# A two-layer decoder trunk on one core: the router's logits and selection taken tile by tile

## The chip, the core and the metric

The kernel runs on one core of a Trainium2 chip (trn2). The metric is the device time of one execution in microseconds (us), and the median of several runs is compared. Names of engines in the rows: PE is TensorE's matmuls, PEld its weight loads, DVE is VectorE, ACT is ScalarE, POOL is GpSimd, SP is the engine that issues the weight loads from HBM, SPq its queue.

## The reference, cut to what matters

Two layers, each on 256 tokens of width 1024. A layer is a token mixer, a cross-attention and a mixture of experts, each followed by a residual sum and a layer norm. The change stands between the second norm and the first expert, so that only this part is quoted:

```python
x = layer_norm(DEEPNORM_ALPHA * x + xa, ln_mem_g[l], ln_mem_b[l])
gates = shared_group_router(x, router_w, router_bias)
ff = moe_ffn(x, gates, expert_w_gate[l], expert_w_up[l], expert_w_down[l])

# in shared_group_router: 16 experts in 4 groups of 4
scores = jax.nn.sigmoid((x @ router_w).astype(jnp.float32))
biased = scores + router_bias.astype(jnp.float32)
grp = biased.reshape(B, S, N_GROUPS, EXPERTS_PER_GROUP)
grp_score = jnp.sum(lax.top_k(grp, TOP_K)[0], axis=-1)
g_sel = jnp.argmax(grp_score, axis=-1)
```

Every token goes to one group of four experts, and to two experts of it. The gates are the scores of these two, divided by their sum.

## The kernel before

**Numbers as two halves.** A float32 value is held as a high half (rounded to fp32r, made by ScalarE as a copy) and a low half (value minus high half, made by VectorE). A product costs three matmuls: high by high, high by low, low by high (`product`, lines 1669 to 1671). A piece of the weights (a "sub" of the stream, 128x1024) goes from HBM into one of 12 slots of `raw`, then ScalarE writes its high half (`split_hi`, line 564) and VectorE its low half (`split_lo`, line 570) into one of 4 slots of `w_split`. The load of sub i waits in `load` for the low half of sub i-12, and the queue of SP is in the order of the stream. `u` in the code is the index of the first of the four subs of expert 0 (U0); u+4 to u+7 are those of expert 1.

**Order of the work.** The order on each engine is written out by hand, as one block of code per engine, and engines meet at semaphores. The 256 tokens are two tiles of 128 (t = 0, 1). The layers are l = 0, 1. Around the router the stages are:

1. VectorE adds the cross-attention output to tile 1 (`add_tile(l, 1)`), scales it, and norms it in two halves (`norm_halves`, line 1256); tile 0 is normed earlier. ScalarE makes the sum of squares (`square`, line 848) and the root between them.
2. TensorE transposes a tile of x (`turn_x` at line 1782 for tile 0, the loop at line 2227 for tile 1), ScalarE and VectorE write the halves `xT_hi` and `xT_lo` of its 1024 features, 512 at a time.
3. `score_tokens(t, h, name)` makes the logits of tile t from the features of half h: four products of `xT_hi` with high and low router weights (128x32, line 2208) and four of `xT_lo` with the high ones (128x16, line 2213). Both tiles go to one bank. Tile 0's second half is scored only after tile 1 has been transposed.
4. ScalarE takes one Exp over the logits of both tiles (line 1020). VectorE makes the sigmoids and picks the group (`router_groups`, lines 1309 to 1330: 14 instructions on both tiles at once, each waiting for the one before by the semaphore `route`). The result `ing` is 1 where a token is in a group.
5. `gather` on TensorE: matmuls with 4 columns number the tokens in a group (line 1975, waiting for `route`; the semaphore is `ranked`). VectorE turns the numbers into one 0/1 matrix for each tile (`place_tokens` at line 1336, `choose` at line 1339, tile `sel`). TensorE gathers the tokens by it: for each of the 8 feature blocks and each tile a product with `xs_hi` and one with `xs_lo` (128x512; lines 1991, 1995, 2001, 2003), where `low_tokens` on VectorE makes `xs_lo` (line 1346).
6. ScalarE and VectorE write the halves `xg_hi` (line 1034) and `xg_lo` (line 1605) of the 8 gathered blocks, and TensorE starts expert 0 (`experts_up`, line 1669), whose sub j waits for block 2j+1. After expert 0 VectorE makes the gates (`router_first`, `router_gates`, up to line 1370), and TensorE's `place_gates` (line 2011) waits for them.

**What TensorE does in between.** In layer 0 it works ahead on the next layer's keys: two subs named MH0 (`half_columns`, 24 matmuls of 256 columns each, operands `memT` and `early`), the first before tile 1 is transposed, the second before the wait for `route`. `kept` is ScalarE's copy of their result. In layer 1 there is no next layer, and `keep_busy(n)` stands in the same places: n matmuls of 512 columns (line 1812) whose result nobody reads.

```python
split_lo(dve, u)
router_groups(l)
place_tokens(l, 0)
choose(l, 0)
place_tokens(l, 1)
over_full(l)
low_tokens(l, 0)
choose(l, 1)
low_tokens(l, 1)
split_lo(dve, u + 1)
split_lo(dve, u + 2)
```

This is VectorE's order from the router to the gathered blocks. `over_full` reads the counts of each group (line 1375).

## Time and profile before

| | us |
|---|---|
| median of 3 runs | 799.74 |
| the runs | 797.49 to 803.34 |
| the profiled execution, its own time | 802.11 |
| its span, first to last instruction | 800.4 |
| busy TensorE in the span | 784.5 |
| busy VectorE | 620.6 |
| busy ScalarE | 511.9 |

The granted clock of TensorE is 0.987 of full speed as a mean over the span. The profile is one execution; its own time is 1.7 us more than its span and 2.4 us more than the median of the runs. Busy time counts an instruction from start to end, and matmuls overlap, so that a busy TensorE may still be working at half its rate. In the timeline a row with xN is N instructions of one kind in a row, with the time from the first start to the last end; a number in brackets is idle time of the engine just before, with what ended it.

### The profile page before, as it was taken

The numbers are of one execution on the slowest core, as the hardware profiler recorded it, in microseconds if no ns is written. First come the engines' busy times: TensorE is split into PE (matmuls) and PEld (weight loads), VectorE is DVE, ScalarE is ACT, GpSimd is POOL, SyncE is SP. The second block draws the span as 40 slices with busy tenths as digits, with TensorE's granted clock in tenths as the row PEclk, the third lists the DMA queues.
The fourth block names the chain that finished last, engine by engine and source line by source line (L and its number), as shares of the span: only waits on it lengthen the run. The fifth ranks groups of instructions, "written<-read, shape, count | busy, mean of one in ns | idle before, by whom it ended". The sixth has DMA issues, their size and how long they took to land.

```text
span 800.4 us, 11973 instructions
## 1 busy us (share of the span) xinstructions
PE 784.5 (98%) x4307; PEld 679.7 (85%) x4307; DVE 620.6 (78%) x1066; ACT 511.9 (64%) x794; POOL 79.4 (10%) x150
## 2 busy tenths in 40 slices
PE   7999999999999999999999999999999999999995
PEld 7999997789888888888899998878988788888884
DVE  4757767694668999999874578768655799999995
ACT  4755565554456788888755567555443668888873
POOL 3169000020000000000011233002000000000000
PEclk9999999999999999999999999999999899999998
DMA  9964433574355799999956543455633459999951
GB/s 312 353 203 157 136 129 132 176 243 122 111 165 140 248 366 370 364 366 372 346 140 194 167 138 131 140 170 172 206 106 106 132 169 359 368 364 368 368 186 54
DMA packets 123118, 177.06 MB, mean 221 GB/s; under 512 B 10176, under 2 KB 92624, under 8 KB 123056
## 3 DMA queue, kind: packets, MB, share of 16 engines
q1 hardware_dynamic: 121072, 169.56, 63.7%
q0 software_dynamic: 1984, 6.70, 2.9%
q8 instruction: 36, 0.59, 0.3%
q14 instruction: 26, 0.21, 0.1%
HBM read 175.18 MB, written 1.05 MB: 220 GB/s over the span
## 4 chain that ended last, share of the span: by engine, by line
PE 89%; DVE 8%; issue 1%; ACT 1%; DMA 1%; DVEq 0%; SPq 0%; ACTq 0%
PE bank L1669 24%; PE bank L1671 24%; PE bank L1670 24%; DVE w_split L570 2%; PE bank L1876 2%; PE bank L1919 2%; PE bank L1910 2%; PE bank L1889 2%; DVE xg_lo L1605 1%; PE bank L1845 1%; PE bank L1865 1%; PE bank L1939 1%; DVE xs L1208 1%; PE bank L1782 1%; PE bank L2029 1%
## 5 line engine op out<-in xcount | busy, mean ns | idle before, releaser
L570 DVE TENSOR_TENSOR w_split<-raw,w_split 128x1024 fp32r<-128x1024 f32 (+3 forms) x334 | 385.2, 1175 | 91.9 <-ACT w_split L564 87.2
L564 ACT ACTIVATE w_split<-raw 128x1024 fp32r<-128x1024 f32 (+3 forms) x334 | 334.8, 1010 | 107.3 <-PE bank L1671 95.2
L1669 PE MATMUL bank<-w_split,xg_hi 128*128 128x512 f32 x256 | 103.0, 403 | 0.1
L1671 PE MATMUL bank<-w_split,xg_lo 128*128 128x512 f32 x256 | 100.2, 391 | 0.0
L1670 PE MATMUL bank<-w_split,xg_hi 128*128 128x512 f32 x256 | 99.9, 390 | 0.0
L1669 PE MATMUL bank<-w_split,xT_hi 128*128 128x384 f32 (+2 forms) x224 | 78.3, 349 | 2.2 <-DVE xT_lo L1135 2.2
L1671 PE MATMUL bank<-w_split,xT_lo 128*128 128x384 f32 (+2 forms) x224 | 76.5, 341 | 0.0
L1670 PE MATMUL bank<-w_split,xT_hi 128*128 128x384 f32 (+2 forms) x224 | 76.4, 341 | 0.0
L1671 PEld LDWEIGHTS bank<-w_split,xg_lo 128*128 128x128 f32 x256 | 48.1, 188 | 10.3
L1669 PEld LDWEIGHTS bank<-w_split,xg_hi 128*128 128x128 f32 x256 | 48.1, 188 | 9.5 <-DVE xg_lo L1605 0.5
L1670 PEld LDWEIGHTS bank<-w_split,xg_hi 128*128 128x128 f32 x256 | 48.2, 188 | 9.0
L1669 PE MATMUL bank<-w_split,mixT_hi 128*128 128x512 f32 x128 | 51.8, 405 | 0.1
L1671 PE MATMUL bank<-w_split,mixT_lo 128*128 128x512 f32 x128 | 50.1, 391 | 0.0
L1670 PE MATMUL bank<-w_split,mixT_hi 128*128 128x512 f32 x128 | 50.0, 391 | 0.0
L1671 PE MATMUL bank<-w_split,aT_lo 128*128 128x512 f32 x128 | 49.8, 389 | 0.0
L1670 PE MATMUL bank<-w_split,aT_hi 128*128 128x512 f32 x128 | 49.8, 389 | 0.0
L1669 PE MATMUL bank<-w_split,aT_hi 128*128 128x512 f32 x128 | 49.8, 389 | 0.0
L1669 PEld LDWEIGHTS bank<-w_split,xT_hi 128*128 128x128 f32 x224 | 42.6, 190 | 2.7 <-DVE xT_lo L1135 2.4
L1670 PEld LDWEIGHTS bank<-w_split,xT_hi 128*128 128x128 f32 x224 | 42.6, 190 | 0.2
L1671 PEld LDWEIGHTS bank<-w_split,xT_lo 128*128 128x128 f32 x224 | 42.6, 190 | 0.1
L794 ACT ACTIVATE qkT<-bank 66x512 f32<-66x512 f32 (+2 forms) x26 | 15.5, 595 | 33.2 <-PE bank L1845 27.0
L1669 PE MATMUL bank<-xT_hi,w_split 128*128 128x256 f32 x112 | 32.4, 289 | 0.0
(325 smaller groups left out, 1521.8 us busy)
## 6 DMA issues: line engine op xcount, KB each, us to landing
raw<-in_expert_w_gate_dram SPq DMA_DIRECT2D x128, 256.0 KB, 5.5
raw<-in_expert_w_up_dram SPq DMA_DIRECT2D x128, 256.0 KB, 7.6
raw<-in_expert_w_down_dram SPq DMA_DIRECT2D x64, 512.0 KB, 7.7
raw<-in_xattn_w_kv_dram SPq DMA_DIRECT2D x32, 512.0 KB, 3.7
raw<-in_w_in_dram SPq DMA_DIRECT2D x40, 384.0 KB, 4.6
raw<-in_w_mix_out_dram SPq DMA_DIRECT2D x16, 512.0 KB, 3.3
raw<-in_xattn_w_q_dram SPq DMA_DIRECT2D x16, 512.0 KB, 3.4
raw<-in_xattn_w_o_dram SPq DMA_DIRECT2D x16, 512.0 KB, 5.3
```

The source lines that it names most:

```text
L564: nc.scalar.activation(halves_of(i)[0][:, 0:w], raw[:, i % RAW, 0:w], ACT.Copy).then_inc(hi_ready, 1)
L570: nc.vector.tensor_tensor(lo[:, 0:w], raw[:, i % RAW, 0:w], hi[:, 0:w].bitcast(F32), ALU.subtract).then_inc(lo_ready, 1)
L794: nc.scalar.activation(qkT[0:d, qk_slot(h), :], B_QK[0:d, :], ACT.Copy).then_inc(qkT_ready.sem, n)
L1208: nc.vector.scalar_tensor_tensor(half, half, ALPHA, product, ALU.mult, ALU.add, accum_out=st[:, 2 * n_ + t, 2 * h:2 * h + 1]).then_inc(sig ...
L1605: nc.vector.tensor_tensor(xg_lo[:, f, :, :].rearrange("p g s -> p (g s)"), bank[XG_BANKS[f]][:, :], xg_hi[:, f, :, :].rearrange("p g s -> ...
L1669: nc.tensor.matmul(o, lhs[0], rhs[0], start=first, stop=False, skip_group_check=shared)
L1670: nc.tensor.matmul(o, lhs[0], rhs[1], start=False, stop=False, skip_group_check=shared)
L1671: return nc.tensor.matmul(o, lhs[1], rhs[0], start=False, stop=last, skip_group_check=shared)
L1876: ins = nc.tensor.matmul(o[:, t * T:(t + 1) * T], qTx[:, 2 * g + c_, t * P:(t + 1) * P], kTx[:, 2 * g + c_, :], start=c_ == 0, stop=c_ == 1)
L1889: ins = nc.tensor.transpose(B_PT[:, k * P:(k + 1) * P], pr[:, k * P:(k + 1) * P], ident[:, :])
L1910: ins = nc.tensor.matmul(B_O[k * HD:(k + 1) * HD, q0:T], v[:, t, g - 1 + k, :], turned_of(h - 1 + k)[:, t * T:t * P + T], start=t == 0, st ...
L1919: ins = nc.tensor.matmul(value_bank(h)[:, dblk * T:(dblk + 1) * T], vx[:, c_, f * P:(f + 1) * P], turned_of(h)[:, c_ * T:(c_ + 1) * T], st ...
```

## The change

The code of each engine between the second norm and the first expert is put in another order, and parts that took both tiles at once are taken per tile.

- **Logits.** `score_tokens` writes tile t into a bank of its own, and its products read 64 columns of each weight half instead of 16: 128 columns (high and low weights) for `xT_hi`, 64 for `xT_lo`. The columns past the first 16 of each half are read by nobody. Both halves of tile 0 are scored before tile 1 is transposed, with a semaphore `first_scored`.
- **Filler.** The matmuls of MH0 (layer 0) are split into pieces of 12, 12, 6, 6 and 12, and `keep_busy` (layer 1) into 8, 4, 6 and 3; before, they were 24 and 24, and 10, 11 and 2 (the 2 in both layers).
- **Transposes.** The one of tile 0 signals its first four blocks too, so that ScalarE starts after them.
- **ScalarE.** One Exp per tile; the copy `xs_hi` of tile 1 before tile 1's Exp; the high half of sub u after both, with those of u+1 to u+3; `kept` after these.
- **VectorE.** `first_sigmoids` (4 instructions on tile 0) between the norm of tile 1 and the low halves of tile 1; `first_groups` takes tile 0 to its group and, interleaved with it, tile 1's sigmoids, so that it waits for tile 1's Exp; then place, choose, low tokens of tile 0; `last_groups` for tile 1; place, choose, `over_full`, low tokens of tile 1. The low half of sub u is made after all that. The low half of `XT0c`'s second 512 features is made before `add_tile(l, 1)`, no longer after tile 1's norm.
- **Gather.** Tile 0's high and low products for 6 of 8 blocks come before tile 1's rank; the other two blocks, whose banks are still in use, follow tile 1's high products. The counts are a third signal of `ranked`, after `sel_ready` of tile 1, and `over_full` waits for it.

The diff, cut to its core:

```diff
-        XG_BANKS = (0, 6, 7, 2, 3, 1, 5, 4)
+        XG_BANKS = (0, 6, 2, 3, 1, 5, 4, 7)
+        EARLY_F = 6
...
+            def score_exp(l, t, signal_):
+                nc.scalar.activation(rt[:, 0::15, t * NE:(t + 1) * NE],
+                                     banks(l, "RT")[t][:, 0:P].rearrange("p (a e) -> p a e", a=2)[:, :, 0:NE],
+                                     ACT.Exp, scale=-1.0).then_inc(signal_.sem, 1)
...
+            def first_sigmoids(l):
+                dve.wait_ge(first_exp.sem, first_exp.at(l, 1))
+                S = columns_of(0)
+                step(nc.vector.tensor_tensor(S[0], S[0], S[15], ALU.mult))
+                step(nc.vector.tensor_scalar(S[1], S[0], 1.0, None, ALU.add))
+                step(nc.vector.reciprocal(S[2], S[1]))
+                step(nc.vector.tensor_tensor(S[3], S[2], rbias[:, :], ALU.add))
...
+            def first_groups(l):
+                group_scores(step, S)
...
+                dve.wait_ge(job_a.sem, job_a.at(l, evac_a[l][job["RT"]]))
+                step(nc.vector.tensor_reduce(first, tied, AX, ALU.max),
+                     nc.vector.tensor_tensor(N[0], N[0], N[15], ALU.mult))
...
             def over_full(l):
-                nc.vector.tensor_scalar(fl[:, 0:NG], bank[5][:, NG:2 * NG], P + 0.5, None, ALU.is_gt)\
+                dve.wait_ge(ranked.sem, ranked.at(l, 3))
+                nc.vector.tensor_scalar(fl[:, 0:NG], bank[4][:, 2 * NG:3 * NG], P + 0.5, None, ALU.is_gt)\
                     .then_inc(counted_over.sem, 1)
...
-                split_lo(dve, u)
-                router_groups(l)
+                first_groups(l)
                 place_tokens(l, 0)
                 choose(l, 0)
+                low_tokens(l, 0)
+                last_groups(l)
                 place_tokens(l, 1)
+                choose(l, 1)
                 over_full(l)
-                low_tokens(l, 0)
-                choose(l, 1)
                 low_tokens(l, 1)
+                split_lo(dve, u)
                 split_lo(dve, u + 1)
                 split_lo(dve, u + 2)
...
+                pe.wait_ge(route.sem, route.at(l, first_at))
+                nc.tensor.matmul(bank[4][:, 0:NG], upto[:, :], ing_r[:, 0:NG], start=True, stop=True)\
+                    .then_inc(ranked.sem, 1)
...
+                pe.wait_ge(sel_ready.sem, sel_ready.at(l, 1))
+                pe.wait_ge(xs_a.sem, xs_a.at(l, 1))
+                for f in range(EARLY_F):
+                    picked(f, 0, xs_hi, True, False)
+                pe.wait_ge(xs_v.sem, xs_v.at(l, 1))
+                for f in range(EARLY_F):
+                    picked(f, 0, xs_lo, False, False)
...
-                        c = slice((kc % 4) * NE, (kc % 4 + 1) * NE)
-                        nc.tensor.matmul(logits[:, o:o + 2 * NE], xT_hi[:, kc, t * P:(t + 1) * P], w_split[:, :, slot, c],
-                                         start=t == 0 and kc == 0, stop=False, skip_group_check=True)
+                        c = slice((kc % 4) * NE, (kc % 4) * NE + 64)
+                        nc.tensor.matmul(logits[:, 0:P], xT_hi[:, kc, t * P:(t + 1) * P], w_split[:, :, slot, c],
+                                         start=kc == 0, stop=False, skip_group_check=True)
...
                 score_tokens(0, 0, "XT0c")
+                score_tokens(0, 1, "XT0c").then_inc(first_scored.sem, 1)
```

How instructions moved on VectorE in layer 1, from the low halves of the transposed x to the matrices `sel`. Names: `rt` is the router's work tile, `ing` the chosen group, `posg` the token's place, `desc_79` the tie-break table, `fl` the counts. Before:

```order
L1135 TENSOR_TENSOR xT_lo<-bank,xT_hi 128x4x128 x3
L570 TENSOR_TENSOR w_split<-raw,w_split 128x1024
L1309 TENSOR_TENSOR rt<-rt 128x32
L1310 TENSOR_SCALAR rt<-rt 128x32
L1311 RECIPROCAL rt<-rt 128x32
L1312 TENSOR_TENSOR rt<-rt,rbias 128x32
```

And in the changed kernel at the same place:

```order
L1329 TENSOR_TENSOR rt<-rt 128x16
L1330 TENSOR_SCALAR rt<-rt 128x16
L1331 RECIPROCAL rt<-rt 128x16
L1332 TENSOR_TENSOR rt<-rt,rbias 128x16
L1151 TENSOR_TENSOR xT_lo<-bank,xT_hi 128x4x128 x2
L1340 TENSOR_TENSOR rt<-rt 128x8
L1341 TENSOR_TENSOR rt<-rt 128x8
```

Tile 0's sigmoids stand ahead of tile 1's low halves, one of the three low halves has gone to an earlier place, and the split of sub u no longer stands ahead of the router.

Also VectorE, layer 1, a little further on: from the last step of the group choice to the gathered blocks (`xg_lo`). Before:

```order
L1330 TENSOR_TENSOR ing<-rt 128x8
L1336 TENSOR_TENSOR posg<-bank,ing 128x4
L1339 TENSOR_TENSOR sel<-iota,posg 128x512
L1336 TENSOR_TENSOR posg<-bank,ing 128x4
L1375 TENSOR_SCALAR fl<-bank 128x4
L1346 TENSOR_TENSOR xs_lo<-xs,xs_hi 128x1024
L1339 TENSOR_TENSOR sel<-iota,posg 128x512
L1346 TENSOR_TENSOR xs_lo<-xs,xs_hi 128x1024
L570 TENSOR_TENSOR w_split<-raw,w_split 128x1024 x2
L1605 TENSOR_TENSOR xg_lo<-bank,xg_hi 128x512 x4
```

In the changed kernel, from the last step of tile 1's group choice:

```order
L1373 TENSOR_SCALAR ing<-rt 128x4
L1379 TENSOR_TENSOR posg<-bank,ing 128x4
L1382 TENSOR_TENSOR sel<-iota,posg 128x512
L1419 TENSOR_SCALAR fl<-bank 128x4
L1389 TENSOR_TENSOR xs_lo<-xs,xs_hi 128x1024
L575 TENSOR_TENSOR w_split<-raw,w_split 128x1024 x3
L1650 TENSOR_TENSOR xg_lo<-bank,xg_hi 128x512 x4
```

Tile 0's place, matrix and low tokens now stand ahead of tile 1's group choice, and three splits instead of two stand ahead of the first `xg_lo`.

TensorE in layer 1, from the logits to the gather (`L2208`, `L2213` and `L2277`, `L2282` are the logits, `memT_hi,ones` is `keep_busy`). Before:

```order
L1812 MATMUL bank<-memT_hi,ones 128x512 x10
L2227 MATMUL bank<-ident,xs 128x128 x8
L2208 MATMUL bank<-w_split,xT_hi 128x32 x4
L2213 MATMUL bank<-w_split,xT_lo 128x16 x4
L2208 MATMUL bank<-w_split,xT_hi 128x32 x4
L2213 MATMUL bank<-w_split,xT_lo 128x16 x4
L2208 MATMUL bank<-w_split,xT_hi 128x32 x4
L2213 MATMUL bank<-w_split,xT_lo 128x16 x4
L1812 MATMUL bank<-memT_hi,ones 128x512 x11
L1975 MATMUL bank<-ing,upto 128x4
```

In the changed kernel:

```order
L1869 MATMUL bank<-memT_hi,ones 128x512 x8
L1837 MATMUL bank<-ident,xs 128x128 x8
L1869 MATMUL bank<-memT_hi,ones 128x512 x4
L2277 MATMUL bank<-w_split,xT_hi 128x128 x4
L2282 MATMUL bank<-w_split,xT_lo 128x64 x4
L2277 MATMUL bank<-w_split,xT_hi 128x128 x4
L2282 MATMUL bank<-w_split,xT_lo 128x64 x4
L2032 MATMUL bank<-ing,upto 128x4
L1869 MATMUL bank<-memT_hi,ones 128x512 x6
L2026 MATMUL bank<-sel,xs_hi 128x512 x6
```

The filler of 11 between the last logits and the first rank is gone, and a part of it stands ahead of tile 1's logits and behind the rank.

## Rows read from the trace of the kernel before

**Rows 1.** the page: busy time by engine, and the chain that ended last

```profile
PE 784.5 (98%) x4307; PEld 679.7 (85%) x4307; DVE 620.6 (78%) x1066; ACT 511.9 (64%) x794; POOL 79.4 (10%) x150
...
PE 89%; DVE 8%; issue 1%; ACT 1%; DMA 1%; DVEq 0%; SPq 0%; ACTq 0%
```

**Rows 2.** windows, layer 0: us, busy PE, PEld, DVE, ACT, POOL; clock; DMA

```profile
243.00:244.00 1.00, 1.00 (x11) 1.00 (x10) 0.89 (x1) 0.08 (x1) 0.00 (x0) 1.00 1.01 377
244.00:245.00 1.00, 1.00 (x7) 1.00 (x7) 0.82 (x4) 0.89 (x2) 0.00 (x0) 0.57 1.35 225
...
247.00:248.00 1.00, 1.00 (x8) 1.00 (x8) 0.19 (x2) 0.00 (x0) 0.00 (x0) 0.73 1.03 366
```

**Rows 3.** windows, layer 1, the same columns

```profile
629.00:630.00 1.00, 1.00 (x10) 1.00 (x10) 0.98 (x2) 1.00 (x2) 0.55 (x2) 0.92 0.16 57
630.00:631.00 1.00, 1.00 (x6) 1.00 (x6) 0.76 (x1) 0.20 (x1) 0.00 (x0) 0.50 0.97 369
...
636.00:637.00 1.00, 1.00 (x6) 0.77 (x5) 0.00 (x0) 1.00 (x2) 0.00 (x0) 0.67 0.00 0
```

**Rows 4.** timeline of TensorE, layer 0: start us, duration us, instruction [idle before]

```profile
237.13 0.37 PE L1669 MATMUL bank<-memT_hi,early 128*128 128x256 f32 x1
...
239.97 0.28 PE L1671 MATMUL bank<-memT_hi,early 128*128 128x256 f32 x1
...
241.25 0.60 PE L2208 MATMUL bank<-w_split,xT_hi 128*128 128x32 f32 x4
...
249.80 1.99 PE L1991 MATMUL bank<-sel,xs_hi 128*128 128x512 f32 x8
```

**Rows 5.** timeline of TensorE, layer 1

```profile
627.30 1.32 PE L2227 MATMUL bank<-ident,xs 128*128 128x128 f32 x8 [0.51 <-DVE xs L1256]
...
632.18 4.84 PE L1812 MATMUL bank<-memT_hi,ones 128*128 128x512 f32 x11
636.86 0.17 PE L1975 MATMUL bank<-ing,upto 128*128 128x4 f32 x1
```

**Rows 6.** timeline of VectorE, layer 0

```profile
236.52 0.69 DVE L1208 SCALAR_TENSOR_TENSOR xs<-xs,bank 128x512 f32<-128x512 f32 x1
...
240.70 2.15 DVE L1135 TENSOR_TENSOR xT_lo<-bank,xT_hi 128x512 fp32r<-128x512 f32 x3
...
248.68 0.16 DVE L1336 TENSOR_TENSOR posg<-bank,ing 128x4 f32<-128x4 f32 x1 [1.46 <-PE bank L1975]
...
252.63 2.35 DVE L570 TENSOR_TENSOR w_split<-raw,w_split 128x1024 fp32r<-128x1024 f32 x2
254.90 2.47 DVE L1605 TENSOR_TENSOR xg_lo<-bank,xg_hi 128x512 fp32r<-128x512 f32 x4
```

**Rows 7.** timeline of VectorE, layer 1

```profile
623.65 0.69 DVE L1208 SCALAR_TENSOR_TENSOR xs<-xs,bank 128x512 f32<-128x512 f32 x1
...
632.62 0.19 DVE L1309 TENSOR_TENSOR rt<-rt 128x32 f32<-128x32 f32 x1 [1.16 <-ACT rt L1020]
...
637.14 0.16 DVE L1336 TENSOR_TENSOR posg<-bank,ing 128x4 f32<-128x4 f32 x1 [1.73 <-PE bank L1975]
...
643.35 2.48 DVE L1605 TENSOR_TENSOR xg_lo<-bank,xg_hi 128x512 fp32r<-128x512 f32 x4
```

**Rows 8.** the router's tile: ns min/median/max, first and last start, forms

```profile
L1311 DVE RECIPROCAL rt<-rt x2: 352/352/353, 244.9 to 633.1; 128x32 f32<-128x32 f32 x2
...
L1321 DVE TENSOR_TENSOR rt<-rt x2: 166/168/169, 245.8 to 634.0; 128x8 f32<-128x8 f32 x2
```

**Rows 9.** timeline of ScalarE, layer 1

```profile
632.36 0.22 ACT L1020 ACTIVATE rt<-bank 128x64 f32<-128x64 f32 x1 [2.16 <-PE bank L2213]
```

**Rows 10.** waits of the whole run: us in total, times, longest

```profile
PEld bank L2011 <- DVE g L1370: 0.4, 2, 0.2
```

**Rows 11.** timeline of the weight queue, layer 0

```profile
244.36 0.37 SPq L505 DMA_DIRECT2D raw<-in_expert_w_gate_dram  x1
...
253.87 0.37 SPq L505 DMA_DIRECT2D raw<-in_expert_w_gate_dram  x1
```

More of the change, by code:

```diff
@@ L1029, in _ @@
                         .then_inc(early_kept.sem, 1)
-                for i in range(u + 1, u + 4):
-                    split_hi(act, i)
                 for f in range(KC):
@@ L1993, in gather @@
-                pe.wait_ge(xs_v.sem, xs_v.at(l, 1))
-                for f in range(KC):
-                    nc.tensor.matmul(bank[XG_BANKS[f]][:, :], xs_lo[:, 0, f * P:(f + 1) * P], sel[:, 0, :],
-                                     start=False, stop=False)
-                pe.wait_ge(sel_ready.sem, sel_ready.at(l, 2))
-                pe.wait_ge(xs_a.sem, xs_a.at(l, 2))
+                    half_columns(l + 1, "MH0", 1, bank[7], (2, 3))
+                else:
+                    keep_busy(3)
@@ new lines, in gather @@
+                pe.wait_ge(sel_ready.sem, sel_ready.at(l, 2))
+                for s in range(TT):
+                    ins = nc.tensor.matmul(bank[4][:, 2 * NG:3 * NG], ones[:, :], ing_r[:, s * NG:(s + 1) * NG],
+                                           start=s == 0, stop=s == TT - 1)
+                ins.then_inc(ranked.sem, 1)
+                pe.wait_ge(xs_a.sem, xs_a.at(l, 2))
+                for f in range(EARLY_F):
+                    picked(f, 1, xs_hi, False, False)
+                if l + 1 < L:
+                    pe.wait_ge(early_kept.sem, early_kept.at(l, 1))
```

184 lines of the change are left out of this document (103 added, 81 removed).

## The prediction, written before the result was known

> **What bounds the kernel now.** I read the page first. TensorE is busy for 98% of the span and makes 89% of the chain that ended last [rows 1]. That invites the reading that whatever frees TensorE shortens the run. Busy is not the same as necessary, though, so the windows of the router's stretch come next. In both layers TensorE stays busy through it, but its granted clock falls from 2.4 to 1.2 GHz: in layer 0 shortly before 244 and until 247 to 248 [rows 2], in layer 1 from just before 630 until 636 to 637 [rows 3]. It had before that done transposes and logit products with 32 and 16 columns for some microseconds [rows 4, 5]. So part of the busy time is slow work, and in layer 1 the 11 `keep_busy` matmuls (4.84 us, [rows 5]) are work that nobody needs.
>
> Third, I read VectorE's timeline in the same stretch, since it makes the group choice, the matrices, the low tokens and the gathered low halves on which expert 0 waits. Between tile 1's residual sum and the first `xg_lo` go 254.90 - 236.52 = 18.38 us in layer 0 [rows 6] and 643.35 - 623.65 = 19.70 in layer 1 [rows 7]. Its large idle times there are one wait of 1.46 in layer 0, for the rank matmul [rows 6], and two of 1.16 and 1.73 in layer 1, for the Exp and the rank [rows 7]. Take these out and 16.92 and 16.81 are left: the same number twice. VectorE works without a real pause, and only those waits can be won. Behind the first `xg_lo` its order is unchanged up to the gates, on which TensorE waits for VectorE in both layers (0.4 in total, [rows 10]). The experts after that are paced by TensorE. So what shifts VectorE's first `xg_lo` shifts the end, and I sum on VectorE.
>
> **The change part by part, on VectorE, per layer.**
>
> *More instructions.* The group choice took 14 instructions on both tiles; now there are 26, 13 per tile. An instruction over 8 columns takes 0.166 to 0.169, one over 32 columns 0.19 (first row of the router in [rows 7]), the reciprocal over 32 columns 0.352 [rows 8, 7]. So the halves cost nearly what the whole did. Before: three of 32 columns at 0.19, the reciprocal 0.35, ten narrow ones at 0.166: 2.6. Now, with 16 columns taken half way (0.175, the reciprocal 0.255), two times 0.78, and 18 narrow ones at 0.165: 4.5. The added hand-overs between dependent steps (8 of 0.04) and the added pairs that overlap (4 by 0.08) cancel. That is +1.9. Bounds: all at the 8-column price 1.8, all at the 32-column price 2.4.
>
> By the Trainium skill ("VectorE: DVE Perf Modes", the section on the TRN2 errata) a fixed latency is paid per instruction, and many small tiles pay it each time, the fixed term being about 150 cycles. An estimate from that page is 12 x 150 / 0.96 GHz = 1.9 us, but it counts only the added instructions. The trace bears the rule out, since a quarter of the columns saves only 0.02 of 0.19.
>
> *A low half moved.* Three low halves of transposed x took 2.15 after the norm [rows 6], 0.72 each; one of them is now made ahead of the residual sum, where VectorE was waiting for TensorE. That is -0.7 in the chain. ScalarE can start after four transposes, not eight, so that the sum starts no more than 0.1 later, in layer 0.
>
> *Small waits.* The three in 2.15 would take 1.9 without gaps, since instructions of 0.69 overlap by some 0.08, and there are two hand-overs from ScalarE around the split of sub u. About 0.4 goes with them.
>
> *Sub u's split.* Two splits take 2.35 [rows 6], about 1.15 each. The one of sub u stood ahead of the router and now stands behind it. Either way it lies between the sum and the first `xg_lo`, so that it costs nothing and wins nothing by itself. Before, though, it filled time in which tile 1's Exp was not ready.
>
> The work is then 16.9 + 1.9 - 0.7 - 0.4 = 17.7, in layer 1 17.6. New waits come on top:
>
> 1. *Tile 1's Exp, asked for in the middle of tile 0's choice.* In layer 0 the sum starts at 236.6, the norm ends 4.1 later (the low halves follow it at 240.70, [rows 6]), then 0.9 of sigmoids, 1.25 for two low halves, 1.2 of group scores: 244.0. TensorE: the transposes of tile 1 end about 241.1; 12 filler products of 256 columns at 0.12 (24 of them between 237.13 and 240.1, [rows 4]) make 242.55; 16 logit products at 0.11 make 244.35; the end of the last one, the Exp (0.22, [rows 9]) and hand-overs make 244.8. VectorE waits 0.8. In layer 1 the filler is only 4 x 0.23, and the same sum gives 631.1 against 631.4: 0.3. The rank of tile 0 is queued behind this wait.
> 2. *Tile 1's rank.* VectorE has nothing between the choice and the place. Matmul to place took 0.28 (636.86 to 637.14, [rows 5, 7]), and the way to TensorE about 0.2: 0.5 in each layer. TensorE is free by then: its 12 products for tile 0 take 12 x 0.23 = 2.7 from the first matrix on.
> 3. *The counts.* `over_full` waits for matmuls that TensorE issues after the filler and after the second matrix. Behind it on VectorE are the low tokens of tile 1, three splits and the first `xg_lo`. In layer 0 the 12 filler products (1.4) end about 251.2, so that it waits 0.8; in layer 1, with 3 x 0.23, 0.5.
>
> Layer 0: 236.6 + 17.7 + 2.1 = 256.4 against 254.90, +1.5. Layer 1: 623.65 + 17.6 + 1.3 = 642.55 against 643.35, -0.8. The sum is **+0.7 us**. The profiled execution took 802.11, 2.4 above the median of 799.74; with the change it should take 802.8, and the median 800.4.
>
> *What this does on TensorE.* The clock's loss and the two spare fillers go, and TensorE ends its gather early: in layer 0 about 255.9, while block 1's low half is ready only at 257.5. It then idles 1.6 ahead of expert 0, and again some 0.8 ahead of its third sub. The gain becomes a wait.
>
> *Logit products.* 128 columns were not run here. The nearest rows are 32 columns at 0.11 (four in 0.60, [rows 4]) and 256 columns at 0.12, so I take 0.11; the far bound is 512 columns, 0.23 (eight in 1.99, [rows 4]).
>
> *Loads.* The load twelve subs on waits for the low half of sub u. It was issued at 244.36, the next one at 253.87 [rows 11]. Both will now go out around 254 to 255, one behind the other. Their subs are split some 20 us later, so this is hidden.
>
> **The rivals.**
>
> *A. TensorE is the bound after all.* For it: rows 1. Then the half clock's loss goes: about 3.4 us long in layer 0 and 6.8 in layer 1 [rows 2, 3], half of it lost, 1.7 + 3.4, and two spare fillers in each layer, 0.9: 6.0, giving 793.8. Against it: the equal 16.9 and 16.8 on VectorE.
>
> *B. The clock falls in the changed stretch too, so that the change does not do what it says.* For it: there are still 8 transposes and 16 narrow logit products in a row, now with idle time on either side. Against it: no stretch without wide matmuls is as long as before. The price: 16 logit products of tile 1 twice as long, +1.8 ahead of tile 1's Exp in each layer, so 0.7 + 3.6 = +4.3: 804.0, slower. It decides wherever the clock falls ahead of tile 1's last logits; later TensorE's 1.6 of idle absorbs most of it.
> By the Trainium skill ("TensorE: Matmul & The Clock Gate", Part 4 on transposes) transposes do not count as a busy array. Then this rival is likelier than the columns alone suggest. In the trace the clock was still full during tile 1's transposes and fell only in the logits, which fits that but does not show it.
>
> *C. Before's usual run does not lose the clock.* The profiled run is 2.4 above the median. If that is the clock, the change repairs what is not broken in the median run. Full clock would take from before's waits about 1.2 in layer 0 (of 1.46) and 2.1 in layer 1 (the 11 fillers in 2.5, not 4.84, and 8 logits). The change is then 0.7 + 3.3 = +4.0: 803.7, slower. Against it: both layers fell in the one run that we see.
>
> *D. Wide logit products at the far bound.* 0.12 more for each of 8 ahead of tile 1's Exp, 0.9 per layer: 802.3.
>
> **How the numbers follow.** Forecast 0.5; A 0.1; B 0.15; C 0.15; D 0.1. The likeliest time is 800.4. Bounds of the unknown costs (the 16-column instructions, the three waits, each 0.2 to 0.3 per layer) are about 1.5 on either side, and the runs of before spread by 2 to 4. The range 797.2 to 804.3 takes in B, C and D and leaves A out. A change of over 1% is 8 us, about what a measurement can tell from none. A reaches 6.0. So faster 0.02, same 0.96, slower 0.02.
>
> **What would show each step right or wrong.** Right: VectorE's distance from tile 1's sum to the first `xg_lo` grows to about 19.8 in layer 0 and shrinks to about 18.9 in layer 1; three new waits of 0.3 to 0.8 at the places named; TensorE idles 1 to 2 us ahead of expert 0, for `xg_lo`; the granted clock stays full. Wrong: no idle time ahead of expert 0 (then A), a window at 0.50 ahead of tile 1's last logits (B), logit products at 0.2 (D), or a wait of a split for its load. The whole is wrong if the first `xg_lo` moves by over 2 us in either layer from what is said.

## The result and the profile after

| | before | after |
|---|---|---|
| median of the runs taken together | 801.29 us (21 runs, 797.36 to 803.51) | 804.25 us (21 runs, 801.37 to 805.48) |
| the profiled execution | 802.11 us | 805.44 us, span 803.7 |

The ratio is 1.0038, with a 95% interval of 1.0026 to 1.0050: the change costs about 3.0 us. The forecast was +0.7. Two things went into the distance between the forecast time, 800.4, and the measured 804.25: the three runs shown of before had their median 1.6 below that of the larger set (799.74 against 801.29), and the change cost 2.3 more than said. One run of all those below, of the new order with narrow products, took 1275.81 us at a mean granted clock of 0.573 and is left out.

The page of the kernel after, its first lines, the clock row and the chain (to hold against [rows 1]):

```profile
span 803.7 us, 11995 instructions
...
PE 783.9 (98%) x4303; PEld 677.3 (84%) x4303; DVE 623.6 (78%) x1090; ACT 512.3 (64%) x796; POOL 79.3 (10%) x150
...
PEclk9999999999999999999999999999999999999998
...
PE 88%; DVE 8%; ACT 1%; issue 1%; DMA 1%; DVEq 0%; SPq 0%; ACTq 0%
```

The page hardly differs from before's. What the change moved stands in two stretches of some 20 us. First VectorE, layer 0 (start, duration, instruction, idle before it with its releaser), as in [rows 6]:

```profile
237.71 0.68 DVE L1224 SCALAR_TENSOR_TENSOR xs<-xs,bank 128x512 f32<-128x512 f32 x1
...
246.15 0.16 DVE L1356 TENSOR_REDUCE rt<-rt 128x1 f32<-128x4 f32 x1 [0.94 <-ACT rt L790]
...
251.47 0.16 DVE L1379 TENSOR_TENSOR posg<-bank,ing 128x4 f32<-128x4 f32 x1 [0.66 <-PE bank L2047]
...
253.06 0.16 DVE L1419 TENSOR_SCALAR fl<-bank 128x4 f32<-128x4 f32 x1 [0.70 <-PE bank L2056]
...
257.68 2.48 DVE L1650 TENSOR_TENSOR xg_lo<-bank,xg_hi 128x512 fp32r<-128x512 f32 x4
```

From the sum to the first `xg_lo` it is 257.68 - 237.71 = 19.97 us, 1.59 more than before. The three idle times are the three new waits: tile 1's Exp, tile 1's rank and the counts. The same view of layer 1, as in [rows 7]:

```profile
626.15 0.68 DVE L1224 SCALAR_TENSOR_TENSOR xs<-xs,bank 128x512 f32<-128x512 f32 x1
...
634.08 0.16 DVE L1356 TENSOR_REDUCE rt<-rt 128x1 f32<-128x4 f32 x1 [0.49 <-ACT rt L790]
...
641.03 0.16 DVE L1379 TENSOR_TENSOR posg<-bank,ing 128x4 f32<-128x4 f32 x1 [2.29 <-PE bank L2047]
...
642.39 0.16 DVE L1419 TENSOR_SCALAR fl<-bank 128x4 f32<-128x4 f32 x1 [0.47 <-PE bank L2056]
...
647.00 1.28 DVE L1650 TENSOR_TENSOR xg_lo<-bank,xg_hi 128x512 fp32r<-128x512 f32 x2
```

Here it is 20.85, 1.15 more than before instead of 0.8 less. Nearly all of the surprise is one number: 2.29 us of waiting for tile 1's rank. TensorE, which makes that rank, in the same stretch (the layer that [rows 5] show of before):

```profile
633.16 0.58 PE L2282 MATMUL bank<-w_split,xT_lo 128*128 128x64 f32 x4
634.71 0.27 PE L2032 MATMUL bank<-ing,upto 128*128 128x4 f32 x1 [0.97 <-DVE rt L1359]
634.84 2.27 PE L1869 MATMUL bank<-memT_hi,ones 128*128 128x512 f32 x6
636.91 2.50 PE L2026 MATMUL bank<-sel,xs_hi 128*128 128x512 f32 x6
639.25 1.55 PE L2026 MATMUL bank<-sel,xs_lo 128*128 128x512 f32 x6
...
640.67 0.25 PE L2047 MATMUL bank<-ing,upto 128*128 128x4 f32 x1
```

And its windows, whose last three columns are the granted clock, the DMA share and GB/s:

```profile
634.00:635.00 1.00, 0.29 (x2) 0.29 (x3) 0.82 (x6) 1.00 (x1) 0.00 (x0) 1.00 1.06 373
635.00:636.00 1.00, 1.00 (x4) 0.82 (x5) 0.93 (x4) 0.99 (x3) 0.00 (x0) 0.79 0.51 168
636.00:637.00 1.00, 1.00 (x4) 0.74 (x3) 1.00 (x2) 1.00 (x2) 0.00 (x0) 0.50 0.00 0
...
639.00:640.00 1.00, 1.00 (x6) 0.80 (x5) 0.00 (x0) 0.28 (x1) 0.00 (x0) 1.00 0.06 16
```

Read the two together. TensorE finishes the logits, idles 0.97 us ahead of tile 0's rank, and within a microsecond after it resumes the clock falls from 2.4 to 1.2 GHz, and stays there for over 3 us. Most of the six fillers and tile 0's six products with `xs_hi` run in that time. Tile 1's rank is queued behind them, so it starts at 640.67, although VectorE had its input ready at 638.74 (the choice of tile 1 starts at 638.51 and takes 0.23). At full clock the same code needs 1.6 less, as the run below without a fall shows.

At the other end TensorE waits, as forecast: 1.29 us ahead of expert 0 in layer 0, 1.30 in layer 1. So in the changed kernel it absorbs nothing more of what VectorE is late. The first row is of after, the second of the same place before:

```profile
259.01 0.50 PE L1714 MATMUL bank<-w_split,xg_hi 128*128 128x512 f32 x1 [1.29 <-DVE xg_lo L1650]
```
```profile
257.06 0.39 PE L1669 MATMUL bank<-w_split,xg_hi 128*128 128x512 f32 x1
```

Before, TensorE did not wait here. It came straight from its last gather product and started expert 0 2.16 us behind the first `xg_lo` (254.90 in [rows 6]); now it starts 1.33 behind it. VectorE had 0.8 us to spare at this point.

### The profile page after: what moved, and what is told of

It is laid out like the page before. It is cut to its first block, busy times and chain, and to the rows that moved or that the text cites. A ratio compares the mean times of both kernels' runs of the same rounds, so it can differ in the third digit from the quotient of the medians.

```text
span 803.7 us, 11995 instructions
## 1 busy us (share of the span) xinstructions
PE 783.9 (98%) x4303; PEld 677.3 (84%) x4303; DVE 623.6 (78%) x1090; ACT 512.3 (64%) x796; POOL 79.3 (10%) x150
## 4 chain that ended last, share of the span: by engine, by line
PE 88%; DVE 8%; ACT 1%; issue 1%; DMA 1%; DVEq 0%; SPq 0%; ACTq 0%
PE bank L1714 24%; PE bank L1716 24%; PE bank L1715 24%; DVE w_split L575 2%; PE bank L1933 2%; PE bank L1976 2%; PE bank L1967 2%; PE bank L1946 2%; DVE xg_lo L1650 1%; PE bank L1902 1%; PE bank L1922 1%; PE bank L2098 1%; DVE xs L1224 1%; PE bank L1996 1%; PE bank L2026 1%
```

## The experiments

Every ratio is to the kernel before, from runs on the same chip. "Distance" is always VectorE's way from tile 1's residual sum to the first `xg_lo`. Where it matters what reaches the end, two more times are read from the profiles: from that sum in layer 0 to the same sum in layer 1, and from there to the end of the span. In two profiles of one kernel they agree to 0.04 us, while the time ahead of the first sum spreads by 2.4 between the profiles. The section on the prediction has them in a table.

### Is VectorE's time the end's time?

Before, with one low half of 128x1024 made a second time behind the router:

```diff
                 split_lo(dve, u + 1)
+                dve.wait_ge(hi_ready, hi_at(u + 2))
+                hi, lo = halves_of(u + 2)
+                nc.vector.tensor_tensor(lo[:, :], raw[:, (u + 2) % RAW, :], hi[:, :].bitcast(F32), ALU.subtract).then_inc(padded.sem, 1)
+                dve.wait_ge(padded.sem, padded.at(l, 1))
                 split_lo(dve, u + 2)
```

> The kernel before, with one low half (128x1024 on VectorE, 1.2 us) made twice, behind the router and ahead of the first xg_lo, in each layer. Theory (VectorE sets the end of the router's stretch): the distance from tile 1's sum to the first xg_lo grows by 1.2 us in each layer and expert 0's later subs start later by nearly as much; time +2.0 to +2.5 us against before. Rival (TensorE is the bound there): the distance on VectorE grows, but TensorE's first matmul of expert 0 and all behind it stay, time +0 to +0.5 us.

Median 802.48, ratio 1.0012 (0.9998 to 1.0026): +1.0 us, between the two, so that the times settle neither. The reason is the base. Before loses clock by different amounts in its own runs: the mean granted clock of 35 runs went from 0.985 (803.2 to 803.9 us) through 0.988 (about 802) to 0.995 (799.3 to 799.5). In this profile layer 1 had the half clock for some 3 us, where [rows 3] have nearly 7, and the pad is lost in that. Layer 0 can be compared, since the half clock lasted 3.4 us there in both profiles. TensorE in this kernel:

```profile
257.51 0.50 PE L1674 MATMUL bank<-w_split,xg_hi 128*128 128x512 f32 x1 [0.24 <-DVE xg_lo L1610]
...
261.04 0.50 PE L1674 MATMUL bank<-w_split,xg_hi 128*128 128x512 f32 x1 [0.49 <-DVE xg_lo L1610]
```

The distance grew by 1.29, to 19.67, and the way to the next layer's sum by 0.97 (387.13 to 388.10). So VectorE's time reaches the end, less some 0.3: TensorE's slack of 0.8 ahead of expert 0 takes a part, and a new wait of 0.49 ahead of the third sub gives most of it back. For the price of a longer VectorE in both layers a base was needed whose clock stays full; the next run gave one.

### The wide logit products alone

```diff
-                    o = 2 * NE * t
+                    o = P * t
...
-                        c = slice((kc % 4) * NE, (kc % 4 + 1) * NE)
-                        nc.tensor.matmul(logits[:, o:o + 2 * NE], xT_hi[:, kc, t * P:(t + 1) * P], w_split[:, :, slot, c],
+                        c = slice((kc % 4) * NE, (kc % 4) * NE + 64)
+                        nc.tensor.matmul(logits[:, o:o + P], xT_hi[:, kc, t * P:(t + 1) * P], w_split[:, :, slot, c],
```

The products with xT_lo go from 16 to 64 columns in the same way, and the Exp reads the columns it needs. The order stays before's.

> The kernel before with the logit products widened to 128 and 64 columns and nothing else; the columns past the first 16 of each part are read by nobody. Theory (the narrow logits make the clock fall, and the fall costs time by lengthening the filler ahead of the rank wait): the granted clock stays full through the router in both layers, the wait for the first rank shrinks from 1.46 to about 0.3 in layer 0 and the waits of 1.16 and 1.73 to about 0.3 and 0.5 in layer 1; time -2.5 to -3.5 us against before. Rival (the clock falls whatever the width, because of the transposes and the short products): windows at 0.50 as before, time within 0.5 us of before. Second rival: a product of 128 columns takes 0.2 us, then +1 to +2 us.

Median 798.64, ratio 0.9972 (0.9957 to 0.9986). A second set of 12 runs of the same kernel:

> The kernel before with the wide logit products alone, once more, as the base for the two padded kernels. Both theories: the same as in its first run, ratio about 0.997 to the kernel before (about 2.2 us faster), the granted clock full through the router's stretch in both layers, distance from tile 1's sum to the first xg_lo 17.4 and 17.3 us.

gave 798.56 and 0.9964 (0.9952 to 0.9977). So this half of the change alone wins 2.2 to 2.9 us, and it beats both kernels. TensorE and VectorE of this kernel in layer 1:

```profile
628.34 0.58 PE L2213 MATMUL bank<-w_split,xT_lo 128*128 128x64 f32 x4
628.75 2.75 PE L1812 MATMUL bank<-memT_hi,ones 128*128 128x512 f32 x11
632.06 0.27 PE L1975 MATMUL bank<-ing,upto 128*128 128x4 f32 x1 [0.56 <-DVE ing L1330]
```
```profile
632.44 0.16 DVE L1336 TENSOR_TENSOR posg<-bank,ing 128x4 f32<-128x4 f32 x1 [0.43 <-PE bank L1975]
...
638.65 1.88 DVE L1605 TENSOR_TENSOR xg_lo<-bank,xg_hi 128x512 fp32r<-128x512 f32 x3
```

The 11 fillers take 2.75 us, not 4.84 as in [rows 5]; the wait for the rank is 0.43, where [rows 6, 7] have 1.46 and 1.73; the distances are 17.38 and 17.31. The clock is full in every microsecond of both stretches. The wide products cost nothing: four of 64 columns take 0.58 here, and four of 128 columns 0.56 to 0.64, while [rows 4] have four of 32 in 0.60. Rival D falls.

That turns the question round. The change holds something that wins over 2 us and still ends at +3.0. Its new order must cost over 5.

### Does the half clock of layer 1 make the long wait?

The kernel after, with four fillers in the gap ahead of tile 0's rank in layer 1:

```diff
                 if l + 1 < L:
                     half_columns(l + 1, "MH0", 1, bank[7], (0,))
+                else:
+                    keep_busy(4)
                 pe.wait_ge(route.sem, route.at(l, first_at))
```

> The changed kernel with four filler matmuls in layer 1 in the 0.97 us in which TensorE idles ahead of tile 0's rank. Theory (that idle time makes the clock fall in layer 1 in most runs, and the fall slows the filler and the first gather ahead of tile 1's rank): the clock stays full in layer 1, the wait for tile 1's rank there shrinks from 2.29 to 0.6 us, and the time is 1 to 2 us below the changed kernel's, that is 1 to 2 us above before. Rival (the narrow logits and the transposes make it fall): the clock falls as before, at most 0.3 us won; four fillers at half clock delay tile 0's rank and cost 0.5 us or more.

Median 803.11, ratio 1.0019 (1.0006 to 1.0033), 1.5 us less than after by the ratios. The wait for tile 1's rank in layer 1 fell from 2.29 to 0.73:

```profile
638.70 0.16 DVE L1379 TENSOR_TENSOR posg<-bank,ing 128x4 f32<-128x4 f32 x1 [0.73 <-PE bank L2049]
```

With the idle time filled, the clock of this profile stayed full in both layers, and the distance in layer 1 came to 19.30, 1.55 less. The way from layer 1's sum to the end fell from 177.55 to 176.02 us, by 1.53, and the one from layer 0's sum to layer 1's is the same (388.44 and 388.47). The long wait was the clock's doing, and it reached the end in full.

### Are the columns what keeps the clock, in the new order too?

The kernel after with the products back at 32 and 16 columns:

```diff
-                        c = slice((kc % 4) * NE, (kc % 4) * NE + 64)
-                        nc.tensor.matmul(logits[:, 0:P], xT_hi[:, kc, t * P:(t + 1) * P], w_split[:, :, slot, c],
+                        c = slice((kc % 4) * NE, (kc % 4) * NE + NE)
+                        nc.tensor.matmul(logits[:, 0:2 * NE], xT_hi[:, kc, t * P:(t + 1) * P], w_split[:, :, slot, c],
```

> The changed kernel with the logit products back at 32 and 16 columns, that is the new order alone. Theory (order and width are two separate terms: the width keeps the clock up and wins about 2.2 us, the order costs about 5): the clock falls in or just behind the logits, at least in layer 1, the waits for tile 1's Exp or rank grow by 1 to 2 us, and the time is 1.5 to 3.5 us above the changed kernel's, 4.5 to 6.5 above before. Rival (the order's mix of fillers keeps the clock up by itself, the width does nothing): within 0.5 us of the changed kernel.

Median of the 11 runs 804.09, ratio 1.0027 (1.0010 to 1.0044): the same as after. So are the two times of the profile, 388.41 and 177.54 against 388.44 and 177.55. Layer 0 keeps its clock with narrow products too; in this order 12 filler products stand between the transposes and the logits. Layer 1 loses it at the same place as after does, behind the same idle time:

```profile
633.41 0.37 PE L2032 MATMUL bank<-ing,upto 128*128 128x4 f32 x1 [0.97 <-DVE rt L1359]
633.64 2.91 PE L1869 MATMUL bank<-memT_hi,ones 128*128 128x512 f32 x6
```
```profile
633.00:634.00 1.00, 0.59 (x2) 0.59 (x3) 0.86 (x6) 0.99 (x2) 0.00 (x0) 0.58 0.81 311
```

A mean of 0.58 in this window means that the half clock began at about 633.2, inside the idle time, and not after it as in after.

So the two parts of the change don't add. In before's order the width cures the clock; in the new order that place keeps its clock with either width, and a new gap opens another.

### The counts, and sub u's split

The kernel after with `over_full` moved behind the low tokens of tile 1:

```diff
                 choose(l, 1)
+                low_tokens(l, 1)
                 over_full(l)
-                low_tokens(l, 1)
```

> The changed kernel with over_full behind tile 1's low tokens on VectorE, where the counts have long been there. Theory (VectorE sets the end, so that each of its waits counts in full): the waits of 0.70 (layer 0) and 0.47 (layer 1) go, the distance from tile 1's sum to the first xg_lo shrinks by as much, time -1.0 to -1.2 us against the changed kernel. Rival (TensorE is the bound): no change in time beyond 0.3 us.

Median 801.77, ratio 1.0016 (1.0002 to 1.0030). The 0.70 and 0.47 of waiting are gone, the distances 19.15 and 18.72. Not all of the 1.8 us won over after belongs to that: this profile also kept its clock in layer 1, with the same idle time as after. Against the kernel with fillers, whose clock was full as well, the ways to the next sum and to the end are 0.88 and 0.52 shorter: 1.4 us for the counts, a little more than expected.

```profile
633.07 0.27 PE L2032 MATMUL bank<-ing,upto 128*128 128x4 f32 x1 [0.97 <-DVE rt L1359]
633.20 1.64 PE L1869 MATMUL bank<-memT_hi,ones 128*128 128x512 f32 x6
634.67 1.54 PE L2026 MATMUL bank<-sel,xs_hi 128*128 128x512 f32 x6
636.06 1.52 PE L2026 MATMUL bank<-sel,xs_lo 128*128 128x512 f32 x6
...
637.44 0.25 PE L2047 MATMUL bank<-ing,upto 128*128 128x4 f32 x1
```

From rank to rank this is 637.44 - 633.07 = 4.37 us, against 640.67 - 634.71 = 5.96 in after: the fall costs 1.6. An idle time of 0.97 is followed by it in some executions and not in others. The runs of after point the same way: seven of 21 have a mean clock of 0.997 and take 801.4 to 802.9 us, the other 14 have 0.992 to 0.995 and take 803.0 to 805.5. The mean also holds the program's start and end, and it doesn't place a fall: the profile of after has 0.995 with the fall, this one has 0.995 without it. So how many of these runs had the fall at this place is an estimate.

The kernel after with sub u's split put back into the wait for tile 1's Exp. On ScalarE its high half goes ahead of that Exp; on VectorE:

```diff
                 step(nc.vector.scalar_tensor_tensor(tied, S[8][:, 0:NG], best, desc4[:, 0:NG], ALU.is_equal, ALU.mult))
+                split_lo(dve, index[l, "U0", 0])
                 dve.wait_ge(job_a.sem, job_a.at(l, evac_a[l][job["RT"]]))
...
                 low_tokens(l, 1)
-                split_lo(dve, u)
```

> The changed kernel with the split of sub u put back ahead of the wait for tile 1's Exp (its high half on ScalarE ahead of that Exp, its low half on VectorE behind tile 0's tie-break). Theory (VectorE's order sets the end, and this wait of 0.94 in layer 0 and 0.49 in layer 1 is filled by the 1.15 us that stand later now): the distance from tile 1's sum to the first xg_lo shrinks by 0.8 to 0.9 in layer 0 and 0.3 to 0.5 in layer 1, time -0.9 to -1.4 us against the changed kernel. Rival (the place of this split does not matter, TensorE is the bound): within 0.3 us of the changed kernel.

Median 803.69, ratio 1.0026 (1.0012 to 1.0040). In layer 0 the distance fell to 19.08, by the 0.9 that the wait for the Exp had taken. In layer 1 the split is longer than the wait, so that tile 0's rank came later, TensorE idled 1.76 ahead of it, and the clock fell, as in the profile of after:

```profile
633.25 0.27 PE L2033 MATMUL bank<-ing,upto 128*128 128x4 f32 x1 [1.76 <-DVE rt L1361]
633.39 2.87 PE L1870 MATMUL bank<-memT_hi,ones 128*128 128x512 f32 x6
```

Its wait for tile 1's rank is 2.28, and its distance 20.52, 0.3 less than after's. So against after the edit won what was expected, 1.0 by the ratios. Against a kernel that keeps its clock it did not: from layer 1's sum to the end it took 177.31 us, and the kernel with fillers 176.02. Eleven of its 12 runs had a mean clock of 0.990 to 0.992, and the one with 0.996 took 800.62 where the others took 802.9 to 805.3. An edit that shortens VectorE's own work lengthened TensorE's idle time, and in layer 1 most of what could be had was lost to the clock.

### All three repairs together

The fillers, the counts and the split in one kernel.

> The changed kernel with the three repairs together: four fillers ahead of tile 0's rank in layer 1, over_full behind tile 1's low tokens, sub u's split in the wait for tile 1's Exp. Theory (the waits add up and what is left is the 1.9 us of added instructions per layer, less 0.7): the distance from tile 1's sum to the first xg_lo is about 18.3 in layer 0 and 18.2 in layer 1 (17.4 and 17.3 in the kernel before with wide logits alone), clock full, time -2.5 to -3.5 us against the changed kernel, within 0.7 us of before, and 1.5 to 2.5 above the wide logits alone. Rival (taking the router tile by tile wins something once its waits are gone): below the wide logits alone.

Median 801.50, ratio 0.9995 (0.9982 to 1.0008): level with before, and 1.8 (by the ratios of this and the first wide set) to 2.9 us (by the medians) behind the wide products in before's order. The clock is full, the distances are 18.89 and 18.72, 0.6 and 0.5 above what was expected. VectorE around its remaining waits in layer 1:

```profile
633.49 0.15 DVE L1358 TENSOR_REDUCE rt<-rt 128x1 f32<-128x4 f32 x1
...
638.85 0.16 DVE L1381 TENSOR_TENSOR posg<-bank,ing 128x4 f32<-128x4 f32 x1 [0.70 <-PE bank L2050]
...
643.47 2.48 DVE L1651 TENSOR_TENSOR xg_lo<-bank,xg_hi 128x512 fp32r<-128x512 f32 x4 [0.26 <-ACT xg_hi L1051]
```

The waits for the Exp and the counts are gone, one for tile 1's rank is left, and the tail now waits a little for ScalarE. What remains against 17.38 and 17.31 is 1.5 and 1.4 per layer. Is that the price of the added instructions, and does it reach the end?

### The price of small instructions

The wide kernel in before's order, with 8 or 16 dependent instructions over 8 columns on VectorE behind tile 0's low tokens. Nothing reads what they write.

```diff
                 low_tokens(l, 0)
+                for i in range(8):
+                    nc.vector.tensor_tensor(R[11 + i % 2][:, 0:8], R[12 - i % 2 if i else 8][:, 0:8], R[8][:, 0:8], ALU.max).then_inc(padded.sem, 1)
+                    dve.wait_ge(padded.sem, padded.at(l, i + 1))
                 choose(l, 1)
```

> The wide kernel with 8 dependent 8-column instructions added on VectorE between tile 0's low tokens and tile 1's selection, in each layer: they compute nothing that is read. Theory (the tiled order costs what its extra instructions cost on VectorE, which sets the end): the distance grows by 8 x 0.19 = 1.5 us per layer to 18.9 and 18.8, which is what the repaired tiled order showed (18.89 and 18.72), and the time rises by 1.2 to 1.5 per layer less the slack TensorE has today, in all 2.0 to 3.0 us over the wide kernel, so that it ends level with the kernel before and with the repaired tiled order (ratio about 1.000). Rival (TensorE's gather bounds the stretch once the clock is full; VectorE has slack): under 1.0 us over the wide kernel, ratio about 0.998.

> The same with 16 added instructions per layer instead of 8. Theory: another 1.5 us per layer with no slack left, so 3.0 us over the kernel with 8 and 5 to 6 us over the wide kernel; ratio about 1.0040 to 1.0045, the distance 20.4 and 20.3. TensorE waits for xg_lo ahead of expert 0 by 1.5 us more than with 8. Rival (slack on VectorE): 1 to 2 us over the kernel with 8.

Eight: median 801.50, ratio 1.0011 (0.9998 to 1.0024), 2.9 us over the wide kernel's 798.56; distances 18.98 and 18.91. Sixteen: 804.87, ratio 1.0050 (1.0031 to 1.0069), another 3.4; distances 20.59 and 20.51. The wide kernel's own are 17.38 and 17.32, so VectorE lost 3.2 us in the two layers together with each step, and the end 2.9 and 3.4. VectorE with eight and with sixteen, layer 0:

```profile
249.54 1.57 DVE L1601 TENSOR_TENSOR rt<-rt 128x8 f32<-128x8 f32 x8
```
```profile
248.98 3.17 DVE L1601 TENSOR_TENSOR rt<-rt 128x8 f32<-128x8 f32 x16
```

A small dependent instruction costs 0.20 us, and with eight of them what VectorE loses the run loses, nearly one for one: the rival, under 1.0 us, falls. The step to 16 shows less than its 3.4 says, since that profile also lost clock in both layers, and the only one of its seven runs with a mean clock of 0.996 took 803.37, 1.9 over the eight. One of the expectations was wrong: TensorE's longer wait with 16 was not for `xg_lo` but for tile 1's low tokens, which lie right behind the pad:

```profile
254.16 0.47 PE L2005 MATMUL bank<-sel,xs_hi 128*128 128x512 f32 x1 [2.50 <-DVE xs_lo L1347]
...
255.16 0.53 PE L2005 MATMUL bank<-sel,xs_hi 128*128 128x512 f32 x1
255.50 0.63 PE L2007 MATMUL bank<-sel,xs_lo 128*128 128x512 f32 x1
...
258.48 0.48 PE L2005 MATMUL bank<-sel,xs_hi 128*128 128x512 f32 x1
```

This gap too was followed by the half clock: the products start 0.43 apart instead of 0.23 until 258.5. With eight the gap was 0.92, and the clock stayed full.

### An earlier low half in before's order

The last part of the change by itself, on top of the wide products: ScalarE starts after four transposes, and both low halves of tile 0's transposed x are made ahead of the sum.

```diff
-                turn_half(l, "XT0c", 0, 0)
+                turn_x(l, "XT0c", 0)
                 wait_job(l, "XO1")
                 add_tile(l, 1)
                 scale(l, 1, 1)
                 norm_halves(l, 1, 1, x_half)
-                turn_half(l, "XT0c", 0, 1)
```

> The kernel before with wide logits and one more part of the change: ScalarE starts on tile 0's transposes after the first four, and VectorE makes both of tile 0's low halves ahead of tile 1's sum. Theory (on VectorE this takes 0.6 out of the chain in each layer, but with wide logits alone TensorE already reaches expert 0 without a wait, 19.5 us after the sum, so that it is now TensorE's fillers and gather that bound): VectorE's distance shrinks by 0.3 to 0.6, TensorE's start of expert 0 by at most 0.3, time -0.5 to +0.2 us against the wide logits alone. Rival (VectorE alone is the bound): -1.0 to -1.3 us against the wide logits alone.

Median 798.63, ratio 0.9953 (0.9936 to 0.9971), with distances 17.39 and 17.30: the same as the wide kernel, whose two medians are 798.64 and 798.56. VectorE then waits 0.7 for ScalarE at tile 1's high half, where the moved low half had stood. By the ratios it would be 0.9 to 1.5 us faster, but the two times of its profile, 386.11 and 174.36, are those of the wide kernel (386.06 and 174.36). So it wins nothing that a profile shows. Since VectorE's distance didn't shrink, this run doesn't tell whether the wide kernel would gain from a shorter one.

## Why the prediction was wrong

**What bounds the stretch: right in the main.** The sum was made on VectorE, and the profiles confirm it. All times are in us, the clock column says in which layers it fell to 1.2 GHz:

| kernel | distance, layer 0 | sum to sum | distance, layer 1 | sum to end | clock fell |
|---|---|---|---|---|---|
| before | 18.38 | 387.13 | 19.70 | 176.75 | 0 and 1 |
| wide products | 17.38 | 386.06 | 17.31 | 174.36 | no |
| after | 19.97 | 388.44 | 20.85 | 177.55 | 1 |
| after with fillers | 19.95 | 388.47 | 19.30 | 176.02 | no |
| counts moved | 19.15 | 387.59 | 18.72 | 175.50 | no |
| sub u's split moved | 19.08 | 387.50 | 20.52 | 177.31 | 1 |
| all three repairs | 18.89 | 387.40 | 18.72 | 175.45 | no |
| wide, 8 instructions added | 18.98 | 387.47 | 18.91 | 175.95 | no |
| wide, 16 added | 20.59 | 389.69 | 20.51 | 177.90 | 0 and 1 |

The distance and the time behind it go together. They do not go one for one, as the prediction's "what shifts VectorE's first `xg_lo` shifts the end" has it. It left out that before TensorE starts expert 0 without a wait, so that the first 0.8 us of VectorE's delay is free there; the new wait ahead of the third sub takes back 0.5. From before to after the distances grow by 1.59 and 1.15, and the times behind them by 1.31 and 0.80. Rival A, TensorE as the bound, falls all the same; TensorE idles 1.29 and 1.30 ahead of expert 0 for `xg_lo` (forecast 1.6), and 0.49 and 0.51 ahead of the third sub (forecast 0.8).

**Layer 0: right.** Forecast 19.8, measured 19.97. The waits: Exp 0.94 for 0.8, rank 0.66 for 0.5, counts 0.70 for 0.8. Take the 2.30 out and 17.67 of work is left, where the forecast had 17.7. In layer 1 it is 20.85 - 3.25 = 17.60, forecast 17.6. So "more instructions +1.9", "a low half moved -0.7" and "small waits -0.4" were right in sum. The Trainium skill's rule ("VectorE: DVE Perf Modes", the TRN2 errata) that many small tiles each pay a fixed latency holds with 0.20 us per dependent instruction in the padded kernels; halving the columns saved almost nothing.

**Layer 1: wrong, and the step that failed is new wait 2, "tile 1's rank ... 0.5 in each layer", with its sentence "TensorE is free by then: its 12 products for tile 0 take 12 x 0.23 = 2.7".** It measured 2.29. The smaller error in it is the size at full clock: 0.7 (0.66, 0.71 and 0.73 in three profiles). The larger is the clock. The forecast had "the granted clock stays full", and it fell for over 3 us on just the work that stands ahead of this rank, the fillers and the first six of the 12 products: 1.6 us. The waits for the Exp (0.49 for 0.3) and the counts (0.47 for 0.5) were about right. On VectorE layer 1 came out 1.95 above the forecast and layer 0 0.17 above.

**From there to the 2.3 us by which the change cost more than said.** At the end layer 1 took 0.8 more than before where the forecast had 0.8 less, and layer 0 1.3 more where it had 1.5: together 1.4 above. Most of the rest is the base. The profile of before is 0.8 above its median, so it had lost more than its usual run, and the change had less to win. The two profiles differ by 3.3; the other 1.2 of that lies ahead of the first sum (237.71 against 236.52), and the profile of after is as much above its own median.

**Rival B was nearly the answer and was priced away.** It had the clock falling in the changed stretch, and named the cause in half a sentence ("now with idle time on either side"). But it looked for the fall ahead of tile 1's last logits, and said of a later one that "TensorE's 1.6 of idle absorbs most of it". That is the wrong engine's slack. TensorE's idle time lies ahead of expert 0, behind VectorE; between the fall and that idle time VectorE asks TensorE for tile 1's rank, so the delay passes to VectorE and from there to the end. The idle time stayed at 1.30. The transposes, which by the Trainium skill ("TensorE: Matmul & The Clock Gate", Part 4) don't count as a busy array, made no difference that could be seen in the profile of after: the clock stayed full through them and through all the logits of both layers. The prediction also misread before: in layer 0 the clock fell not "shortly before 244" and in the logits but just behind 244 ([rows 2] have 1.00 until then), in the filler products behind them; only in layer 1 did it fall in the logits.

**Rival C fell, but for a part.** Before does lose clock in its usual run: its profiled 802.11 lies only 0.8 above the median of 21 runs. The 2.4 that C rested on came from a median of three. The 0.8 is what is left of it. Nine of the 21 runs took less than 800 us, and in the sets with a clock on record all runs of before under 800 have a mean of 0.994 or 0.995; for those C may hold.

**What the change gave and took.** Measured against the wide kernel in before's order, whose distances are 17.4 and 17.3, the changed kernel's are 2.6 and 3.5 longer, 6.1 in all; the ratios differ by 0.0066 to 0.0074, 5.3 to 5.9 us. In the two times of the table they are 2.4 and 3.2 longer, 5.6. Of the 6.1, the repaired kernel keeps 2.9: the added instructions net of the moved low half, a longer wait for the rank (0.70 for 0.43) and the new one for ScalarE. The repairs take away 3.2: 1.2 for the counts, 1.6 for the clock where it falls, and the rest, 0.4, for the waits for the Exp (1.43 in both layers) net of the new waits. Against that stands the clock that before lost and the change keeps, 2.2 to 2.9 us, which wider products keep as well without a new order.

**Open.** Why 0.97 us of idle time is followed by the half clock in some executions and not in others; whether moving the counts changed that or was lucky in its profile. Why tile 1's sum in layer 0 comes between 235.28 and 237.71 in the profiles; the latest is that of after, and two profiles of the same wide kernel have 235.28 and 236.91. And whether a shorter VectorE would still shorten the wide kernel, in which TensorE starts expert 0 without a wait.

## What to carry to other kernels

Price each half of a change alone: a widening of a few lines held all the gain here, and the reordering around it took it back twice over. When work is split by tile, count instructions, not columns, and on every in-order queue that makes something for the bound engine list all that stands ahead of it, fillers too. Then look at the bound's far end: if the next engine doesn't wait there yet, its slack is to be taken off first. Look for idle times of TensorE that a new order opens between stretches of heavy work, and ask who waits for the matmuls behind them: there a lost clock is paid, and slack further on does not take it up.

## What the hardware showed that was not expected

- Short idle times went with the half clock: 0.97 us in the profile of after and in that of its narrow kernel, 1.76 in that with sub u's split moved, and 2.50 in both layers of the profile with sixteen added instructions. Others were not: 0.97 in one profile, 0.92 in that with eight added instructions, and the 1.29 and 1.30 ahead of expert 0. So the length of the gap alone doesn't decide it; no run here separates what else does. Nor is a gap needed: before lost the clock in layer 0 without any idle time of TensorE in the 6 us ahead. In four of the five cases the fall began 0.2 to 1.1 us after work resumed, in the narrow kernel 0.2 before that, and it lasted over 3 us each time, so that the work behind the gap pays.
- The time of a product with few columns did not depend on their number: four in about 0.6 us for 16, 32, 64 and 128 columns.
- Identical code spread by 2 to 4 us from one run to the next. In before this went with the clock (799.5 at a mean of 0.995, 803.5 at 0.985), but not everywhere: with eight added instructions the two slowest runs, 802.84 and 803.21, had the highest mean, 0.997. The wide kernel varied less in its second set: 797.3 to 799.1, where before had 798.4 to 803.6 beside it.
